# An fp32 kernel of two transformer blocks: rotary by a lane shuffle, routing by token halves, the sigmoid on ACT, one weight split later

## The reference, cut to what matters

```python
def layer_norm(x, g, b, eps=1e-5):
    xf = x.astype(jnp.float32)
    mu = xf.mean(-1, keepdims=True)
    var = jnp.square(xf - mu).mean(-1, keepdims=True)
    return ((xf - mu) * lax.rsqrt(var + eps) * g + b).astype(x.dtype)

# hierarchical_moe: 4 groups of 8 experts, the best group, then its two best experts
    g_logits = (x @ w_rg).astype(jnp.float32) + b_rg
    grp = jnp.argmax(g_logits, axis=-1)
    e_all = jnp.einsum('nd,gde->nge', x, w_re).astype(jnp.float32) + b_re
    e_logits = jnp.take_along_axis(e_all, grp[:, None, None], axis=1)[:, 0]
    top_val, top_idx = lax.top_k(e_logits, TOP_K)
    gate = jax.nn.softmax(top_val, axis=-1) * p_grp
...
        return (jax.nn.silu(xb @ w_gate[e]) * (xb @ w_up[e])) @ w_down[e]
```

```python
def apply_rope(x, cos, sin):
    xf = x.astype(jnp.float32)
    half = xf.shape[-1] // 2
    x1, x2 = xf[..., :half], xf[..., half:]
    return jnp.concatenate([x1 * cos - x2 * sin, x2 * cos + x1 * sin], axis=-1).astype(x.dtype)
```

## Time and profile before

| what | value |
|---|---|
| time, median of 3 runs | 754.43 us (753.81 to 759.05) |
| the profiled execution | 761.98 us, of which 760.2 from the first to the last instruction |
| mean granted clock of PE in it | 0.952 |
| PE busy | 682.1 us, 90% |
| DVE busy | 368.4 us, 48% |
| ACT busy | 324.3 us, 43% |
| POOL busy | 16.8 us, 2%, 31 instructions |
| moved by DMA | 167.80 MB |

### The profile page before, as it was taken

The page is one execution under the profiler, slowest core; times in us unless marked ns, Lnnn a source line. Parts: engine busy times, 40 slices in busy tenths (PEclk is TensorE's granted clock), DMA queues, the critical chain, the costliest instruction groups (busy, mean ns, idle before and its releaser), DMA issues.

```text
span 760.2 us, 11653 instructions
## 1 busy us (share of the span) xinstructions
PE 682.1 (90%) x4580; PEld 520.5 (68%) x4582; DVE 368.4 (48%) x813; ACT 324.3 (43%) x759; POOL 16.8 (2%) x31
## 2 busy tenths in 40 slices
PE   6989999996599999798796799999979999999986
PEld 4968998695343455264251388878859898888876
DVE  1633657445432132021121456678775466787733
ACT  2565665421000112020120243678865545788742
POOL 5001000000000000000000000000000000000000
PEclk9999999898589999898989899999999999999999
DMA  9967331399959999999999729008163080073301
GB/s 280 340 201 246 111 112 56 123 302 367 315 223 350 414 410 414 415 409 416 414 410 411 251 88 300 1 1 274 61 221 111 1 274 5 1 231 103 111 1 56
DMA packets 94616, 167.80 MB, mean 221 GB/s; under 512 B 4238, under 2 KB 75648, under 8 KB 90464
## 3 DMA queue, kind: packets, MB, share of 16 engines
q1 hardware_dynamic: 92272, 160.88, 59.0%
q0 software_dynamic: 2160, 6.07, 2.3%
q10 hardware_dynamic: 128, 0.08, 0.0%
HBM read 165.93 MB, written 1.07 MB: 220 GB/s over the span
## 4 chain that ended last, share of the span: by engine, by line
PE 72%; SPq 11%; DMA 5%; ACT 5%; DVE 4%; issue 2%; ACTq 0%; DVEq 0%
PE psum L851 13%; PE psum L853 11%; PE psum L852 11%; SPq L741 9%; PE psum L1206 4%; PE psum L1247 4%; PE psum L894 4%; PE psum L1145 3%; DMA ring<-in_w_expert_down_dram 3%; PE psum L1261 3%; PE psum L1192 2%; DMA ring<-in_w_expert_up_dram 2%; PE psum L986 2%; PE psum L1104 2%; PE psum L1233 1%
## 5 line engine op out<-in xcount | busy, mean ns | idle before, releaser
L851 PE MATMUL psum<-a_high,w_high 128*128 128x256 f32 x512 | 150.9, 295 | 2.1 <-ACT q_c L1472 1.3
L853 PE MATMUL psum<-a_high,w_low 128*128 128x256 f32 x512 | 144.7, 283 | 0.0
L852 PE MATMUL psum<-x_low,w_high 128*128 128x256 f32 x512 | 144.6, 283 | 0.0
L2187 DVE TENSOR_TENSOR w_low<-ring,w_high 128x1024 fp32r<-128x1024 f32 (+1 forms) x79 | 111.2, 1421 | 23.4 <-ACT w_high L1572 23.3
L851 PEld LDWEIGHTS psum<-a_high,w_high 128*128 128x128 f32 x512 | 97.7, 191 | 13.8 <-issue 4.7
L1572 ACT ACTIVATE w_high<-ring 128x1024 fp32r<-128x1024 f32 (+1 forms) x79 | 95.9, 1219 | 9.6 <-DMA ring<-in_w_in_dram 6.2
L852 PEld LDWEIGHTS psum<-x_low,w_high 128*128 128x128 f32 x512 | 97.8, 191 | 0.4
L853 PEld LDWEIGHTS psum<-a_high,w_low 128*128 128x128 f32 x512 | 97.8, 191 | 0.0
L851 PE MATMUL psum<-w_high,a_high 128*128 128x256 f32 x240 | 69.6, 290 | 0.0
L852 PE MATMUL psum<-w_low,a_high 128*128 128x256 f32 x240 | 68.5, 285 | 0.0
L1247 PE MATMUL psum<-ring,q_c 128*32 128x512 f32 x320 | 55.1, 682 | 11.0 <-DMA ring<-in_w_expert_up_dram 7.0
(11 more groups left out here) (334 smaller groups left out, 1190.4 us busy)
## 6 DMA issues: line engine op xcount, KB each, us to landing
ring<-in_w_in_dram SPq DMA_DIRECT2D x36, 1024.0 KB, 8.7
ring<-in_w_expert_down_dram SPq DMA_DIRECT2D x24, 1024.0 KB, 18.0
ring<-in_w_expert_gate_dram SPq DMA_DIRECT2D x40, 512.0 KB, 14.6
ring<-in_w_expert_up_dram SPq DMA_DIRECT2D x40, 512.0 KB, 15.3
ring<-in_w_out_dram SPq DMA_DIRECT2D x12, 1024.0 KB, 5.1
ring<-in_w_mem_kv_dram SPq DMA_DIRECT2D x4, 1024.0 KB, 16.5
k_c<-in_w_expert_gate_dram SPq DMA_DIRECT2D x5, 512.0 KB, 14.9
k_c<-in_w_expert_up_dram SPq DMA_DIRECT2D x5, 512.0 KB, 15.9
```

What stands on the lines that cost most here:

```text
L851: pe.matmul(dst, left[0], right[0], start=first, stop=False)
L852: pe.matmul(dst, left[0], right[1], start=False, stop=False)
L853: return pe.matmul(dst, left[1], right[0], start=False, stop=last)
L2187: dve.tensor_tensor(w_l, raw_of(n), as_f32(w_h), ALU.subtract).then_inc(lows, 1)
```

## The change

- **Rotary.** The job `swap` is no longer a job of PE. DVE fetches the partner rows itself by a stream shuffle within 32 lanes, multiplies by sin, and adds the product with cos, which POOL has made in one of two buffers (`cosined`: the router weights' buffer and the constants of `places`, both free by then). POOL starts as soon as ACT has taken the tile and the rotary tile two before is done.
- **Routing.** The jobs are now, for each half of the tokens, two transpositions with one half of the columns each, and a logit job with x as the stationary operand, whose result has tokens in the rows: `logitT` is gone. The bias comes as a row for all partitions.
- **Choice and rank.** Compare and multiply are one instruction per token half; the mask is one small operation and two additions. PE signals `ranked` after the products that DVE needs, and counts after that, in another bank. The penalty for experts that were not chosen is made while PE ranks. The first gather needs only the places; gates and weighted places come later.
- **Sigmoid.** ACT does exp(-x), ln(1 + .), exp(-.), linked by semaphores; DVE's addition and reciprocal are gone.
- **End of the experts.** The closing matmuls have 64 columns. The third weight part of the second block is split later: by ACT at the job ("mk", 0, 1), by DVE behind the second layer norm.

```diff
-TAKEN_BY_DVE = ("bias", "xt2", "y1", "logit", "logitT", "rank", "swap")
+PARTNER = [(m + 16) % 32 for m in range(32)]
+TAKEN_BY_DVE = ("bias", "xt2", "y1", "logit", "rank")
...
-    jobs += [("x1t", k) for k in range(4)] + [("logit",), ("logitT",), ("rank",)]
+    for tt in range(2):
+        jobs += [("x1t", tt, 0), ("x1t", tt, 1), ("logit", tt)]
+    jobs += [("rank",)]
...
+            for n, (l, t) in enumerate(ROPES):
+                pool.wait_ge(p_act, taken(JOB[("tile2", l, t)]))
+                if n >= 2:
+                    pool.wait_ge(roped, n - 1)
+                pool.tensor_tensor(cosined[n % 2], tile3[:, t, :], c_("cos_lin" if t < 6 else "cos_ax"), ALU.mult
+                                   ).then_inc(cosine, 1)
...
                 elif kind == "x1t":
-                    pe.wait_ge(ln_done, 2)
-                    mm = turn4(dst, x4, job[1])
+                    tt, half = job[1:]
+                    pe.wait_ge(ln_done, tt + 1)
+                    for c in range(4):
+                        mm = pe.transpose(dst[:, P * c:P * c + P], x4[:, tt, 4 * half + c, :], ident)
                 elif kind == "logit":
-                    from_act(("x1t", 3))
+                    tt = job[1]
                     pe.wait_ge(router_in, 16 * (1 + GROUPS))
                     for k in range(KC):
-                        mm = pe.matmul(dst[0:GROUPS + EXPERTS, 0:T], router[:, k, :], xT3[:, k, :],
+                        if k % 4 == 0:
+                            from_act(("x1t", tt, k // 4))
+                        mm = pe.matmul(dst[:, 0:GROUPS + EXPERTS], xT3[:, k, P * tt:P * tt + P], router[:, k, :],
                                        start=(k == 0), stop=(k == KC - 1))
...
-                elif kind == "swap":
-                    l, n = job[1:]
-                    from_act(("tile2", l, n))
-                    mm = pe.matmul(dst[:, 0:T], swap, tile3[:, n, :], start=True, stop=True)
...
             def experts():
-                pe.wait_ge(p_dve, taken(JOB[("rank",)]))
                 pe.wait_ge(setup, 2)
-                pe.wait_ge(placed, 1)
+                pe.wait_ge(located, 1)
                 gather_half(0, 0)
+                pe.wait_ge(p_dve, taken(JOB[("rank",)]))
...
-                    mm = pe.matmul(bank(b), zeros_b[:, 0:P], zeros_b[:, :], start=False, stop=True, skip_group_check=True)
+                    mm = pe.matmul(bank(b)[:, 0:64], zeros_b[:, 0:P], zeros_b[:, 0:64], start=False, stop=True,
+                                   skip_group_check=True)
...
-                act.activation(gate_e, bank(6)[:, 0:DE], ACT.Exp, scale=-1.0).then_inc(gate_exped, 1)
+                then(act.activation(gate_e, bank(6)[:, 0:DE], ACT.Exp, scale=-1.0))
+                then(act.activation(gate_e, gate_e, ACT.Ln, bias=1.0))
+                act.activation(gate_e, gate_e, ACT.Exp, scale=-1.0).then_inc(gate_exped, 1)
...
+            def rope(l, n):
+
+                tl = tile3[:, n, :]
+                m = rope_nth(l, n)
+                if m > 1:
+                    dve.wait_ge(roped, m - 1)
+                dve.wait_ge(p_act, taken(JOB[("tile2", l, n)]))
+                link(dve.stream_shuffle(rope_a, tl, PARTNER))
+                op = dve.tensor_tensor(rope_a, rope_a, c_("sin_lin" if n < 6 else "sin_ax"), ALU.mult)
+                dve.wait_ge(cosine, m)
+                link(op)
+                op = dve.tensor_tensor(tl, cosined[(m - 1) % 2], rope_a, ALU.add)
+                if n >= 12:
+                    dve.wait_ge(p_act, taken(JOB[("hsq", l, n)]))
+                    link(op)
+                    op = dve.tensor_tensor(tl, tl, sq_tile(n), ALU.mult)
+                op.then_inc(roped, 1)
...
-                link(dve.tensor_tensor(score3, values3, wide(best), ALU.is_equal))
-                link(dve.tensor_tensor(score3, score3, order, ALU.mult))
+                for tt in range(2):
+                    op = dve.scalar_tensor_tensor(score3[:, tt], values3[:, tt], best[:, tt:tt + 1], order,
+                                                  ALU.is_equal, ALU.mult)
+                link(op)
...
+            def locate_first(src):
+
+                dve.wait_ge(ranked, 1)
+                link(dve.tensor_tensor(rank, src[:, 0:2 * EXPERTS], e_sc, ALU.add))
+                for tt in range(2):
+                    op = located_in(0, None, tt)
+                op.then_inc(located, 1)
...
-                then(dve.tensor_scalar(gate_e, gate_e, 1.0, None, ALU.add))
-                then(dve.reciprocal(gate_e, gate_e))
                 then(dve.tensor_tensor(gate_e, gate_e, bank(6)[:, 0:DE], ALU.mult))
...
             def experts():
-                places(0, None, link)
+                gates_of()
+                dve.wait_ge(located, 1)
+                weigh(0)
                 back_copy(0, backs[0])
...
-                for n in AT_EXPERTS:
+                for n in AT_EXPERTS[0:2]:
                     low(n)
                 dve.wait_ge(moe_done, 1)
...
                 scaled(1, 1)
+                low(AT_EXPERTS[2])
```

More of the change, by code:

```diff
@@ L241 @@
 TURNS = schedule()
-JOBS = [job for jobs, _ in TURNS for job in jobs]
+JOBS = [job for jobs, _ in TURNS for job in jobs if job[0] != "swap"]
+ROPES = [job[1:] for jobs, _ in TURNS for job in jobs if job[0] == "swap"]
 JOB = {job: n for n, job in enumerate(JOBS)}
@@ L1364, in _ @@
                 for job in jobs:
+                    if job[0] == "swap":
+                        continue
                     run(job, j)
@@ L2269, in _ @@
                 for job in jobs:
+                    if job[0] == "swap":
+                        rope(*job[1:])
+                        for n in lows_now:
+                            low(n)
+                        lows_now = []
+                        continue
                     if job == ("cnat", 0):
```

162 lines of the change are left out of this document (79 added, 83 removed).

## The result

The changed kernel takes 751.25 us (median of 20 runs; the ratio leaves out one of 2139 us and one of 757.02 us, which was in a slow state), the kernel before 758.51 in the same comparison; the ratio is 0.9893, with an interval of 0.987 to 0.9916. Two later comparisons gave 0.9875 (0.9837 to 0.9914) and 0.9844 (0.9799 to 0.9888). So the change makes the kernel 8 to 12 us faster by these ratios, where 19.4 were forecast. The kernel before had a median of 758.5 to 759.7 us in all comparisons; the 754.43 from which I subtracted came from three runs.

A forecast was written before the change was run, and what follows sets the result against it. The weights' stream was taken to bound the experts, PE the second block's layers. Terms 8.5 + 0 + 0.85 + 10.0 = 19.35 us, subtracted from 754.43, gave 735.0 us (742.6 for the profiled execution); range 727 to 745.

The forecast's parts named there:

- Parts 1 and 2: Routing: x turned and routed by token halves, and a shorter choice and rank; 6.8 to 10.9 us, taken as 8.5.
- the two clocks: Routing up to the logits: 3.9 us sooner at PE's slow rate, 8.0 us at its fast rate.
- Part 3: Experts' sigmoid moved to ACT: 1.2 us less from gate to hidden, but nothing counted in the total.
- Part 4: End of the experts: closing matmuls cut from 512 to 64 columns save 0.85 us; moving the third split gives nothing.
- Part 5: Second block's two layers: rotary swaps taken off PE by a DVE shuffle save 5.0 us per layer, 10.0 in both.
- Rival A: Second block's steps: DVE and ACT take PE's place, only the openings' rotary share stays; 739.3 us, chance 0.18.
- Rival D: Second block: POOL's product and DVE's two-input instructions shut each other out, 35 us on DVE's path; 770 us, chance 0.05.

The follow-up runs named there:

- old_sigmoid: The changed kernel with the experts' sigmoid using DVE's addition and reciprocal again; ratio 0.9890 against 0.9893 for the changed kernel.
- rope_later: The changed kernel with tile 14's rotary chain two steps later in the schedule; 742.78 us, 6.9 us below the changed kernel beside it.
- cos_dve: The changed kernel with the cosine product on DVE in place of GpSimd; ratio 0.9871 against 0.9875.
- lows_first: The changed kernel with the weight split's low half ahead of the rotary chain on DVE, in steps where one is due; 748.8 us, ratio 0.9846.
- warm: The changed kernel with small products of zeros in four PE waits of each second-block layer; 746.33 us against 749.63 for the changed kernel beside it.

## Why the prediction was wrong

**Parts 1 and 2 (8.5 us) were right.** From the last addition of the first block to the first gather the four profiles of kernels with the old routing take 25.8 to 26.2 us, the fourteen with the new one 17.3 to 19.4, on average 18.3: 7.75 us less. In the changed kernel's profile the logits lie in SBUF at 186.63, 10.95 us behind the last addition, where they took 16.57: 5.6 us, between the two clocks as taken. From logits to chosen 0.6 were won where 0.9 were expected, from there to the gather 1.96 where 2.0 were (0.9 and 1.1). That the stream takes it in whole was right too: from the last addition to tile 0 the same two sets average 277.25 and 269.5 us, 7.7 apart.

**Part 3 (0) was right**, by old_sigmoid. **Part 4 (0.85) can't be told from zero.** The instructions shrank by 0.75 us, but the stretch they lie in varies by 6 us.

**Part 5 (10.0 us) is the step that failed.** The opening was right: between the copies of tile 0 and tile 5 exactly 2.90 us go (17.30 to 14.40), in every profile with the shuffle; by tile 8, behind the opening's fifth swap and the first of the steps', it is 3.74, where 3.98 were expected (2.9 + 0.45 + 0.63). What failed is the term for the other four swaps of the steps, "I count 60% of these, 1.5", with the 0.5 us put down for DVE's delays: 1.0 us to be won in each layer. Measured on the copies, they lose 0.6 us even where the clock stays up: 0.4 by tile 9 and 0.2 by tile 19 (15.79 became 16.0). So a layer gains 3.1 us at full clock and not 5.0. Then comes what the sum had no term for, the drop in the wait, 1.5 us in 11 of 16 layers. Rival A's mechanism was this one, but its price was too low: in it the four swaps bring nothing, here they cost. DVE and ACT not only took PE's place, the order of DVE's queue put tile 20's low half behind a rotary chain that was never wanted so early. I had read 28.6 of 33.2 us of DVE as a share. It should have been read at the place where a low half ends just as PE asks for it: 525.78 plus half of 2.35, against PE's 527.15. That slack was 0.2 us. The eight profiles with the wait gain between 0.5 and 8.1 us in the two layers, on average 3.3; rope_later gains 9.4. That this is nearly the 10.0 that I had put down is in part luck: up to tile 19, where no drop comes into it, the rotary part with the chain moved gives 4.2 us per layer (3.74 - 0.4 + 0.9), 8.5 in both, and the rest is the clock at the layers' ends. Those ends also took 1.5 and 1.3 us from the changed kernel's first profile, by the clock alone.

**Rival D** was wrong in its price, as I held, but its mechanism is there. The Trainium skill ("SBUF — State Buffer", "Who interferes with whom") says that a two-input DVE instruction and a GpSimd instruction that reads SBUF exclude each other. The trace agrees. GpSimd's timeline in layer 0, and DVE's beside it:

```profile
451.61 0.75 POOL L855 TENSOR_TENSOR const<-tiles,const 128x256 f32<-128x256 f32 x1 [2.13 <-ACT tiles L1479]
454.49 1.47 POOL L855 TENSOR_TENSOR router_w<-tiles,const 128x256 f32<-128x256 f32 x1 [2.13 <-ACT tiles L1479]
457.36 1.13 POOL L855 TENSOR_TENSOR const<-tiles,const 128x256 f32<-128x256 f32 x1 [1.41 <-ACT tiles L1479]
```

```profile
453.26 0.42 DVE L1900 TENSOR_TENSOR q_c<-q_c,const 128x256 f32<-128x256 f32 x1
...
454.13 1.22 DVE L2230 TENSOR_TENSOR w_low<-ring,w_high 128x1024 fp32r<-128x1024 f32 x1
...
455.76 0.48 DVE L1900 TENSOR_TENSOR q_c<-q_c,const 128x256 f32<-128x256 f32 x1
```

A product took 0.72 to 0.76 us by itself. The one of 454.49 began 0.86 us before a split ended and took 1.47: it ended 0.6 us behind the split, and so did the other products that began in the first 1.1 us of a split. In the other direction, a multiplication by sin that began 0.2 us before a product's end took 0.48 us and not 0.42 (eight of the 20; a ninth, begun 0.3 us before it, took 0.58). No split began during a product, and the splits kept their mean of 1422 ns. So here GpSimd does nearly all the waiting, and it has the time: without it (cos_dve) the ratio is the same.

**The base.** 4 of the 16 us between 735 and 751.25 come from subtracting from a median of three runs. Worked from the profiled execution the forecast was 742.6, and the changed kernel's profiled execution took 748.26. The sum was 19.4 and 8 to 12 came: by the means of the profiles 6.7 us are missing in part 5 and 1.6 in parts 1 to 4, which would leave 11.1. What the times lack of that in two of the three comparisons is, by the estimate above, in part the clock of those runs; the rest stays open.

## What to carry to other kernels

Where work is taken off the bounding engine, look for the first place where another engine's result arrives with less slack than the work that goes, and take what isn't awaited out of that engine's queue there, to a place where it has time. Changing places within the same step was not enough (lows_first); two steps later was (rope_later). Here one line of the schedule made a gain of 1.1 to 1.6% into one of 2.2%. Count a new wait of TensorE at what it adds to the stretch (here 1.1 of its 2.0 us) plus the slow clock that may follow it, and read more than one profile, at the same events, before a difference of 1% is explained.

## What was not expected of the hardware

- The same program, profiled twice, had first layers of 150.23 and 153.99 us with the same instructions and the same wait of 2.0 us before tile 20: only the granted clock differed, 1.00 against 0.88 and 0.78 in the two slices there, and 1.00 against 0.94 behind the last tile. A single profile can hide or make up a gain of 4 us in a stretch of 150.
- The runs' times follow the mean granted clock. The changed kernel's runs in the first comparison go from 745.33 us (0.958) and 745.77 (0.967) to 755.35 (0.943), the two outliers left out.
- A stream shuffle of 128 by 256 in fp32 took 0.44 us on DVE, as long as a two-input multiplication (0.42).
- Products of zeros in bf16, whose result nobody reads, stood in the wait of 2 us in the run warm, and the clock stayed at 1.00 in both layers; unfilled, it fell in 11 of 16. That is one profile.
- A GpSimd product of two inputs that begins while DVE subtracts two operands in SBUF ends 0.6 us behind that subtraction (0.75 us became 1.00 to 1.47).
